# Hybrid Hawk / Mamba-2 / PEER layer on one core: score products made in four portions between the query blocks

## What is computed

```python
def block(tb):                                   # tb: tokens x 1024
    q = (tb @ w_q).reshape(blk, PEER_HEADS, 2, PEER_HALF)        # 16 query blocks of 128
    s = jnp.einsum('thsk,hsnk->thsn', q, sub_keys)               # 16 x 128 scores a token
    sv, si = lax.top_k(s, PEER_TOPK)
    cand = sv[:, :, 0, :, None] + sv[:, :, 1, None, :]
    ...
    fv, fi = lax.top_k(cand.reshape(blk, PEER_HEADS, PEER_TOPK * PEER_TOPK), PEER_TOPK)
    idx = jnp.take_along_axis(cand_idx..., fi, axis=-1)
    g = jax.nn.softmax(fv, axis=-1)
    act = jax.nn.gelu(jnp.einsum('thkd,td->thk', u_emb[idx], tb))
    return jnp.einsum('thk,thkd->td', (g * act), v_emb[idx])
```

## Time and profile before

| | us |
|---|---|
| median of 3 runs | 2330.93 |
| lowest and highest | 2326.48, 2336.44 |
| the profiled execution, its time | 2352.97 |
| its span, first to last instruction | 2351.2 |
| PE busy in the span | 1711.3 (73%) |
| DVE busy | 1556.3 (66%) |
| POOL busy | 918.6 (39%) |
| ACT busy | 540.0 (23%) |

### The profile page before, as it was taken

The page is one execution under the profiler, slowest core; times in us unless marked ns, Lnnn a source line. Parts: engine busy times, 40 slices in busy tenths (PEclk is TensorE's granted clock), DMA queues, the critical chain, the costliest instruction groups (busy, mean ns, idle before and its releaser), DMA issues.

```text
span 2351.2 us, 30749 instructions
## 1 busy us (share of the span) xinstructions
PE 1711.3 (73%) x10511; PEld 1183.2 (50%) x10511; DVE 1556.3 (66%) x4092; ACT 540.0 (23%) x1574; POOL 918.6 (39%) x840
## 2 busy tenths in 40 slices
PE   7999977687898898987899879996534434343433
PEld 7899976443587776765577667663100000000000
DVE  4634178777578547888756776435388878877855
ACT  4446255100135123432122341111001000010000
POOL 0000001156434454543454455555644454444442
PEclk8999999757799999997899999997655566566566
DMA  6487767289999999986799899987999999999995
GB/s 226 148 269 251 249 198 266 81 307 405 398 398 381 402 409 359 359 312 215 275 379 349 337 388 388 401 336 289 397 421 422 421 417 421 417 415 413 414 421 234
DMA packets 181932, 798.79 MB, mean 340 GB/s; under 512 B 20977, under 2 KB 21233, under 8 KB 147857
## 3 DMA queue, kind: packets, MB, share of 16 engines
q0 software_dynamic: 119808, 570.48, 61.7%
q1 hardware_dynamic: 59616, 219.40, 25.6%
q10 hardware_dynamic: 2352, 6.95, 1.0%
HBM read 779.88 MB, written 12.14 MB: 337 GB/s over the span
## 4 chain that ended last, share of the span: by engine, by line
PE 20%; DMA 14%; DVE 11%; issue 5%; POOL 3%; ACT 0%; another core or an unknown queue 0%; POOLq 0%; DVEq 0%; ACTq 0%; SPq 0%
PE ps L490 11%; DMA s_exr<-in_uv,s_gidx 6%; DMA s_wr<-in_uv,s_gidx 3%; PE ps L817 3%; DVE s_exr L1722 2%; PE ps L800 2%; PE ps L473 2%; DMA s_scr<-in_uv,s_gidx 2%; DMA s_hnr<-in_uv,s_gidx 1%; DMA s_exr<-in_v,s_gidxT 1%; POOL s_exr L1379 1%; DVE s_wr L1722 1%; DVE s_scr L1722 1%; PE ps L839 0%; POOL s_exr L1365 0%
## 5 line engine op out<-in xcount | busy, mean ns | idle before, releaser
L490 PE MATMUL ps<-s_hnr,s_wr 128*128 128x256 f32 (+2 forms) x3968 | 679.9, 330 | 48.5 <-ACT s_hist_p L978 24.5
L490 PEld LDWEIGHTS ps<-s_hnr,s_wr 128*128 128x128 f32 x3968 | 610.3, 197 | 128.0 <-issue 73.8
L1334 POOL DMA_INDIRECT s_exr<-in_u,s_gidx x288 | 310.2, 1077 | 838.3 <-DVE s_act_z L1722 449.3
L1722 DVE CUSTOM_DVE_ANT_0 s_exr<-s_exr,s_tbg 128x1024 f32<-128x1024 f32 x407 | 491.7, 1221 | 167.1 <-DMA s_exr<-in_u,s_gidx 100.1
L1346 POOL DMA_INDIRECT s_exr<-in_v,s_gidxT x256 | 279.4, 1091 | 197.8 <-issue 89.8
L817 PE MATMUL ps<-s_exr,s_sw 128*32 128x512 f32 x476 | 156.5, 1044 | 164.0 <-DVE s_sw L1751 164.0
L1379 POOL DMA_INDIRECT s_exr<-in_uv,s_gidx x119 | 140.3, 1179 | 149.2 <-PE ps L817 120.9
L800 PE MATMUL ps<-s_exr,s_zb 128*32 128x512 f32 x1072 | 152.7, 659 | 41.6 <-DMA s_exr<-in_v,s_gidxT 29.6
L1427 DVE SCALAR_TENSOR_TENSOR s_scr<-s_scr,s_par 128x128 f32<-128x128 f32 (+2 forms) x288 | 122.2, 426 | 50.3 <-ACT s_scr L984 41.5
L817 PEld LDWEIGHTS ps<-s_exr,s_sw 128*32 128x32 f32 x476 | 25.0, 157 | 244.0 <-DVE s_sw L1751 191.6
L1157 ACT ACTIVATE s_gth<-s_g 128x4 f32<-128x4 f32 x64 | 13.1, 205 | 566.3 <-DVE s_g L1740 566.3
(11 more groups left out here) (314 smaller groups left out, 2695.6 us busy)
## 6 DMA issues: line engine op xcount, KB each, us to landing
s_wr<-in_wstream SPq DMA_DIRECT2D x360, 512.0 KB
s_tbg<-s_h2e ACTq DMA_DIRECT2D x36, 128.0 KB
s_exr<-in_u,s_gidx POOLq DMA_INDIRECT x288
s_exr<-in_v,s_gidxT POOLq DMA_INDIRECT x268
s_xr<-in_sample_h_in SPq DMA_DIRECT2D x8, 512.0 KB, 7.9
s_scr<-in_sample_h_in SPq DMA_DIRECT2D x8, 512.0 KB, 7.3
out_sample_h_out<-s_xr SPq DMA_DIRECT2D x8, 512.0 KB
out_sample_h_out<-s_scr SPq DMA_DIRECT2D x8, 512.0 KB
```

Of the source, the lines that this page charges most:

```text
L490: last = pe.matmul(ps[:, o % 2, 0:n], wring[:, slot, k, :], rhs[:, k, :], start=k == 0, stop=k == KT - 1)
L1334: pool.indirect_dma_start(uring[n % URING], None, a["u"], bass.IndirectOffsetOnAxis(ap=gidx[:, i % 2, s:s + 1], axis=0)).then_inc(u_in[n % ...
L1722: dve.tensor_tensor_reduce(out=u, in0=u, in1=tbg[:, i % 2, :], scale=1.0, scalar=0.0, op0=ALU.mult, op1=ALU.add, accum_out=act_z[:, i % 2, ...
```

## The change

`scores(pc, i, q)` now makes the products of one query q, over all groups of 32 tokens. It is called twice behind unit 4i+2 (q = 0 and 1), once behind unit 4i+3 (q = 2) and once behind unit 4i+4 (q = 3; for the last block behind unit 15). Each portion waits only for its own query block, the first one of a block also for `sc_ready`, and the last one sets `sc_mm`. The products are the same ones. In a portion all of them go to the same 32 PSUM partitions, that is to the same quarter of the array's columns.

```diff
-            def scores(pc, i):
-
-                pe.wait_ge(q_ready, 16 * pc.p + 4 * (i + 1))
-                if i:
+            def scores(pc, i, q):
+
+                hs = (2 * q + i // 2) * 2 + i % 2
+                pe.wait_ge(q_ready, 16 * pc.p + 4 * i + q + 1)
+                if i and q == 0:
                     pe.wait_ge(sc_ready, 4 * pc.p + i)
                 for g in range(pc.ngr):
-                    for q in range(4):
-                        hs = (2 * q + i // 2) * 2 + i % 2
-                        last = pe.matmul(ps[GT * q:GT * (q + 1), 2 + g // 4, (g % 4) * NKEYS:(g % 4 + 1) * NKEYS],
-                                         pc.qs[:, q, GT * g:GT * (g + 1)], pc.keys[:, hs, :], start=True, stop=True)
-                last.then_inc(sc_mm, 1)
+                    last = pe.matmul(ps[GT * q:GT * (q + 1), 2 + g // 4, (g % 4) * NKEYS:(g % 4 + 1) * NKEYS],
+                                     pc.qs[:, q, GT * g:GT * (g + 1)], pc.keys[:, hs, :], start=True, stop=True)
+                if q == 3:
+                    last.then_inc(sc_mm, 1)
...
-                    if n >= RINGW and n % RINGW == 0:
-                        scores(pc, n // RINGW - 1)
+                    if n % RINGW == 2:
+                        scores(pc, n // RINGW, 0)
+                        scores(pc, n // RINGW, 1)
+                    elif n % RINGW == 3:
+                        scores(pc, n // RINGW, 2)
+                    elif n and n % RINGW == 0:
+                        scores(pc, n // RINGW - 1, 3)
                     pace.after(pc, "wq", n)
-                scores(pc, HS // RINGW - 1)
+                scores(pc, HS // RINGW - 1, 3)
```

## The result

The changed kernel took 2366.3 us (5 runs, 2365.3 to 2369.57), the kernel before 2330.93 us. The ratio is 1.0152, with a 95% interval of 1.0136 to 1.0169: 35.4 us slower. The profiled execution of the changed kernel took 2366.3 us, as long as its median run. That of the kernel before, from which the earlier trace rows are, was 22 us longer than its own median. This turned out to matter: the two profiles differ by 13.3 us only, while the runs differ by 35.4. A time of 2384 us, which the prediction gave for a profile of the changed kernel, did not appear.

A forecast was written before the change was run, and what follows sets the result against it. The prediction took PE to bound all three `wq` stages. Its terms, 11.9 + 12.3 + 7.0 = +31.2 us on the median of 2330.93 us, gave 2362 us, with a range of 2340 to 2382 us.

The forecast's parts named there:

- The price of the portions: Score products in all three pieces: 0.113 us a record, serial on one quarter, plus 0.2 us a visit.
- both gains: Piece 2: portions would neither starve after 46 records nor leave holes after which the clock falls; old cost counted 24.1 us.
- rival 3: Piece 2: starving belongs to the profiled execution or goes on, so counted gains fall away; 16 us more, +47, 2378 us; chance 0.10.
- the gains at L529: Piece 1, wait behind the scores: shrinks from 3.81 to 2.49 us, 1.3 us off; piece 0's 2.49 us wait stays.
- Piece 0: First `wq` stage, 128 records: 16.7 us after against 4.8 before, +11.9 us, all passed on.
- Piece 1: Second `wq` stage, 160 records: 20.3 us after against 6.7 before, less 1.3 us of shorter wait, +12.3 us.
- Piece 2: Third `wq` stage, 256 records: 31.1 us after against 24.1 before, +7.0 us.
- ACT's wait for the scores: ACT before its copy of the scores: 43.6 us in 8 cases would shrink, worth 0 to the total.
- Rival 1: Second `wq` stage: the full DMA covers the added PE time, leaving +18.9 us, 2350 us; chance 0.13.
- rival 2: Score portions: products still overlap at 0.032 us a record, so 11.6 us less than before, 2319 us; chance 0.08.
- Rival 4: Score portions: the clock falls as only a quarter of the array works, 25 us more, 2387 us; chance 0.06.
- Rival 5: Score portions: the weight load is not hidden, 544 x 0.110 = 60 us more, 2422 us; chance 0.03.

The follow-up runs named there:

- e9: Changed kernel with every score product made twice, one behind the other: 2425.3 us, 1.0399 against the kernel before.
- e10: Kernel before with the change in piece 1 alone, its score products made twice, old runs in pieces 0 and 2: 2356.3 us, 1.0112 against before.
- e6: Kernel before with only the order in each score run changed, query outside and group inside, old place: 2361.3 us, 1.0024 against before.
- e11: Same kernel as e6, repeated beside a kernel before that takes 2330.9 us: 2348.4 us, 1.0074 against before.
- e7: Changed kernel, but queries 0 and 1 together behind unit 4i+2, 2 and 3 behind 4i+4, query inside: 2358.3 us, 1.0014 against before.
- e12: The changed kernel unaltered, measured a third time: 2360.9 us, 1.0132 against the kernel before at 2330.9 us.
- e4: Kernel before with the change in piece 2 alone, old runs in pieces 0 and 1: 2361.6 us, 1.0033 against before.
- e1: The kernel before, unaltered, once more with a profile of its own: 1.0015 against the kernel before, which took 2351.6 us.
- e8: Kernel before with piece 2's packed score run cut in two, groups 0 to 3 in the middle of unit 4i+4, the rest behind it: 1.0005 against before.
- third comparison: e9, e10, e11 and e12 measured on one chip beside the kernel before, which took 2330.9 us there.
- second comparison: e5, e6, e7 and e8 measured on one chip beside the kernel before, which took 2356.2 us there.
- e5: The changed kernel unaltered, measured again: 2377.5 us, 1.0098 against the kernel before at 2356.2 us.

## Why the prediction was right, and where its terms were off

The forecast was 2362 us, the result 2366.3. The mechanism was right: products on one quarter run one behind the other, PE is the bound in all three stages, and what it does more comes out at the end. e9 and e10 show the last part, e6 with e11 and e7 the first. But two terms of the sum were off by more than 10 us each, in opposite directions. That the total came within 4.2 us is luck.

**The price of the portions was too high.** I took 0.113 us a record and 0.2 us for each of 33 visits, 68.1 us in all. The steps of the timeline add up to 13.2, 16.6 and 27.7 us, 57.5 in all. A record costs 0.109 us (16 records 1.86 us, 8 records 0.99), a visit 0.12 us. (The visits are 34: in piece 2 `values` stand between the last two portions.) What I did not see coming is the pair: two portions right behind each other on different quarters take 1.45 instead of 2 x 0.99 us, 1.89 instead of 2 x 1.21, 3.21 instead of 2 x 1.86. Each time 0.51 to 0.53 us are saved. Of these 0.12 us are the second visit, which a pair does not make, and 0.4 us the switch of quarters. e11 agrees: 32 records on four quarters in one visit take 2.39 us, where 32 x 0.109 + 0.12 make 3.61, so each of the three switches saves 0.41 us. The 0.52 us a switch that I expected for e6 were too much.

**The gain in piece 2 was none where the kernel before takes 2331 us.** The step that failed is "here I count both gains for the change". It was put as rival 3, that the starving belonged to the profiled execution, with 16 us. e10 shows the packed stage without it: 77.2 us, so stage 2 costs 97.1 - 77.2 = 19.9 us (e12 against e10) and not 7.0. The profile before had 95.0 us there, 17.8 more than e10, which is most of the 22 us by which it was longer than its median. Only on the two chips where packed runs starve do the 7 us come near the truth (7 to 14 in e4). Rival 3 was right as to the size of the gain (16 us, against 17.8), but not as to the total of +47 us, since the portions and L529 took less. And it was only half right as to the cause: e1 starved again, so it is no matter of one execution but of the chip or the moment.

**The sum made anew.** The changed portions take 57.5 us; the packed runs, without starving, 4 x (1.01 + 1.23 + 1.88) = 16.5 us. That is +41.0. Off it go the gains at L529, which the changed kernel no longer makes at half clock behind a longer wait: it waits 1.77 and 1.82 instead of 2.49 and 3.81 us, and lasts 2.37 and 3.54 instead of 3.96 and 5.1 us to the next record; together 5.9 us. 35.1 us remain, against 35.4 and 30.0 (26 to 35) measured in the two comparisons in which the kernel before took 2331 us. I had counted 1.3 of these 5.9 us; the clock was missing. (The wait, too, was another: it ends with DVE's `HN`, not with ACT's copy.) At L529 the granted clock was 0.50 to 0.87 before and 1.00 after. Why it fell there is not shown by the length of the wait: L529 ran at the full clock behind 2.34 and 2.50 us in e7 and 2.79 us in e8, and at half clock for most of it behind 2.21 us in e10.

**The parts of it.** In the third comparison order alone costs 17.5 us (e11). Cutting the runs into portions between the units costs the rest, 2360.9 - 2348.4 = 12.5 us. The timelines agree with the second part: the serial runs in one place take 4 x (2.39 + 3.26 + 5.88) = 46.1 us, 11.4 us less than the portions, and L529 waits 1.9 us less in e11. For the first part they give more than was measured: 46.1 - 16.5 = 29.6 us, less 7.7 us at L529, is 21.9 us. These 4 us stay unexplained. In the second comparison, where the kernel before starves, the same two parts were 5 and 16 us.

**Point by point.** Piece 0: +11.9 forecast, some 8 by the table. Piece 1: +12.3 forecast, some 7. Piece 2: +7.0 forecast, 3.8 between the first two profiles, 19.9 without starving. ACT's wait for the scores, which I expected to shrink, went from 43.6 to 48.2 us; no run separates what that is worth. The wait for `sc_ready` cost 1.21 us once. Rival 1 (DMA covers) is ruled out by e9 and e10, rival 2 (the products still overlap) by the 60.0 us. Rival 4 (the clock falls) did not come about: the granted clock was 1.00 in the portions.

```profile
1552.40:1555.60 3.20, 3.20 (x39) 3.14 (x40) 1.23 (x2) 0.68 (x3) 2.56 (x3) 1.00 1.00 374
1578.40:1581.70 3.30, 3.30 (x35) 3.06 (x33) 0.00 (x0) 0.66 (x3) 2.39 (x4) 1.00 0.98 335
```

(Stretches of the changed kernel: length; busy time and records of PE, PEld, DVE, ACT, POOL; granted clock; DMA share; GB/s.) Rival 5, by the rule of the Trainium skill (TensorE: Matmul & The Clock Gate, Part 3), is refuted. All these products use the same rows, the weight load lasts 110 ns in the rows of L779, and yet a record costs 0.109 us and not 0.22. The measurement decides. Another sentence of that part of the Trainium skill lets a weight load also be pulled ahead when it targets a background weight buffer; with that the number agrees.

**What stays open.** Why PE stands idle at "issue" on two of the chips and not on the third. The profile shows no difference in the transfers of instructions: q8 carries 85 packets with 0.2% of the DMA time both in the profile before and in e12. It is not the length of a run (e8) and not the packing alone (e6 starved in serial runs). In all profiles of the changed kernel its portions had no hole, and neither had piece 2 of e4, but in e4 and e5 PE waited for "issue" elsewhere. No version was found that beats the kernel before; e7 and e8 are equal to it within 0.4%, both on a chip where it starves.

## What to carry to other kernels

In this kernel a product that fills only 32 columns of the array cost a quarter of a full one only while four of them, on four quarters, stood behind each other in the program. Keep the loop over the quarter innermost. If work must be spread, spread it by token groups (e8, equal to before) rather than quarter by quarter; pairs of quarters (e7) cost twice the PE time of four. Before a difference in stall time is counted as a gain, see whether another profile of the same kernel has the stall at all: here the profile was 22 us longer than the median run, and that was the warning.

## What the runs showed of the hardware

- fp32 products with 128 moving columns and 32 weight columns: with four quarters in turn each further record cost 0.027 us (32 in 1.01 us, 64 in 1.88, e10), with two quarters 0.054 (16 in 1.00 us, 32 in 1.87, e7), with one 0.109 (8 in 0.99 us, 16 in 1.86). The weight load of 0.110 us is hidden in all three. What is left over in such a row, 0.12 to 0.14 us, is read here as the price of one visit to the 32-wide form.
- Each switch to another quarter right behind a row of products on one quarter saved about 0.4 us (pairs of portions, and the runs of e11).
- L529 was made at a granted clock of 1.00 behind waits of up to 2.79 us (e8) and at 0.59, the mean of 3 us, behind one of 2.21 us (e10).
- The same kernel took 2331 us on one chip and beside the changed kernel in the result above, and 2352 to 2356 us on two others. The visible part of it is PE's time at "issue": 3.2 to 3.7 us in the four profiles of that chip, none of which is of the kernel before, and 22 to 41 us in the eight of the others.
